# Expert stage with gate and up taken chunk by chunk together

## The chip, the cores and the metric

One core of one Trainium2 chip runs the whole program. The metric is device time in microseconds (us) from start to end of one execution.

## What is computed

The reference runs two layers over 288 tokens, 256 of a prompt and 32 of samples, with 1024 features each. A layer mixes the tokens (retention and a causal convolution) and then sends each token to two of 16 experts. An expert is a gated product with three 1024 x 1024 matrices of its own in float32:

```
ys = (silu(xb @ w_gate[e]) * (xb @ w_up[e])) @ w_down[e]      # for a block xb of tokens
```

The two results of a token are added with the router's weights, scaled by a gate of the layer and added to the residual. The change touches only this expert stage.

## The kernel before

The rows of an expert are taken in blocks of 64 (the kernel's own size), so the 576 pairs of token and expert make 16 experts with one or two blocks each, 35 blocks over both layers. A block is a pass through a loop on each engine; the engines meet at semaphores.

**Weights.** SP loads everything through a ring of twelve slots (line 133). A unit is two chunks of 128 rows of a 1024-wide matrix, 128 x 2 x 1024 floats. Slots 0 to 3 hold gate, 4 to 7 up, 8 to 11 down. SP issues the units in program order and waits for each unit's slot, `freed[s]`, before it issues it (lines 367 to 374). Before the first expert of a layer the same slots hold modulation weights: part 3 in slots 0 to 3 (line 359), part 4 and then part 5 in slots 4 to 7 (lines 360 and 366), w_out in 8 to 11. Slots 4 to 7 are given back by PE in the modulation slab at line 692, late in the mixing stage. After an expert's units SP waits for `routed` and reads the number of its blocks (lines 376 to 378). A slot is given back once per block, and a unit of the next expert waits until the last block of this one has used its slot. Behind the last expert of layer 0, SP loads modulation weights of layer 1 into slots 0 to 7 and convolution weights into 8 to 11 (lines 379 to 387).

**A block on PE** (lines 785 to 834). `half_products` (line 756) is one chunk of one matrix: two matmuls, one for each 512 columns, that write the two halves of a PSUM bank; in float32 each is two instructions. A block is: eight chunks of gate into bank 2; behind the fourth, the combines 0 to 2, which put the result of the block before into banks for DVE to add; eight chunks of up into bank 3, with combine 3 behind the first; `gather` of the next block's rows; the transposes of `hs`, which wait for `h_act`; the transposes of `selT` and `xtok`; eight chunks of down into bank 0. PE gives a slot back behind its last chunk, apart from the last slot of each matrix: ACT gives back slot 3 behind `gate_done` (line 1007) and slot 11 (line 1014), DVE gives back slot 7 behind `up_done` (line 1458).

**ACT and DVE.** ACT takes the sigmoid of gate (line 1008), with a table load before it in each block, then copies rows and results. DVE builds the selections of the next block, takes the combines into the residual (`take`, line 1423), makes the first product of gate and sigmoid (line 1454), then take(3), then the second product with up (line 1460), which signals `h_act`.

In the rows, the helpers stand for most operations: line 406 is every matmul, 409 every transpose, 875 every ACT operation, 374 every load of an expert's unit.

Of the kernel before, what the change touches and what calls it, by code (L numbers as in the profile page):

```python
# [13 lines left out]
KC = D // P  # L14
# [15 lines left out]
UK = 2  # L30
UQ = KC // UK
# [89 lines left out]
def hybrid_step_kernel(nc, x_prompt, x_sample, state_ret, state_conv, c_prompt, c_sample, w_mod, b_mod, g_mix_norm,  # L121
# [6 lines left out]
    with ctx:  # L128
# [99 lines left out]
        xg = cut("moe", 512)  # L228
# [58 lines left out]
        V = type("Signals", (), S)  # L287
# [17 lines left out]
        @block.sync  # L305
        def _(sp):
            mod_v = w_mod.rearrange("l (q k p) c -> l q p k c", q=UQ, p=P)
            in_v = w_in.rearrange("l (q k p) c -> l q p k c", q=UQ, p=P)
            out_v = w_out.rearrange("l (q k p) c -> l q p k c", q=UQ, p=P)
            exp_v = [w.rearrange("l e (q k p) c -> (l e) q p k c", q=UQ, p=P) for w in (w_exp_gate, w_exp_up, w_exp_down)]  # L310

            def row_loads():
                for row, n, src in ((R_GMIX, 8, g_mix_norm), (R_GFFN, 8, g_ffn_norm), (R_BMOD, NMB, b_mod), (R_BCONV, 4, b_conv),
                                    (R_GCLN, 4, g_conv_ln), (R_BCLN, 4, b_conv_ln), (R_GRET, 4, g_ret_gn)):
                    sp.dma_start(vrows[row:row + n, :, :], src.rearrange("l (r p) -> r l p", p=P)).then_inc(in_rows, 16)
                for l in range(L):
                    sp.dma_start(vrows[R_GFIN:R_GFIN + 8, l, :], g_final.rearrange("(r p) -> r p", p=P)).then_inc(in_rows, 16)

            for j in range(2):
                for q in range(UQ):  # L320
                    s = j * UQ + q
                    sp.wait_ge(freed[s], 1)
                    sp.sem_inc(tick, 1)
                    sp.dma_start(ring[:, s], mod_v[0, q, :, :, (1 - j) * D:(2 - j) * D]).then_inc(loaded[s], 16)
                    if s == 1:
                        row_loads()
            blk = sp.alloc_register("blocks_before")
            sp.reg_mov(blk, 0)

            def conv_load(layer, uses):  # L330
                for q in range(UQ):
                    s = G_CONV * UQ + q
                    sp.wait_ge(freed[s], uses(s))
                    sp.sem_inc(tick, 1)
                    sp.dma_start(ring[:, s], in_v[layer, q, :, :, 2 * D:3 * D]).then_inc(loaded[s], 16)

            conv_load(0, lambda s: 1)
            sp.dma_start(cbt[0:120, :, :], state_conv.rearrange("l b t c -> l (b t) c").rearrange("l (r p) c -> l p r c", p=120)[0]) \
                .then_inc(cb_first, 16)
            sp.dma_start(cst[:, NFIRST:], consts[:, NFIRST:]).then_inc(in_const, 16)  # L340
            for l in range(L):

                b0 = sp.snap(blk)
                for j in (G_QK, G_VG):
                    for q in range(UQ):
                        s = j * UQ + q
                        sp.wait_ge(freed[s], unit_uses(s, l, 0, b0))
                        sp.sem_inc(tick, 1)
                        sp.dma_start(ring[:, s], in_v[l, q, :, :, j * D:(j + 1) * D]).then_inc(loaded[s], 16)

                def mod_load(group, k, layer, part):
                    for q in range(UQ):
                        s = group * UQ + q
                        sp.wait_ge(freed[s], unit_uses(s, l, k, b0))
                        sp.sem_inc(tick, 1)
                        sp.dma_start(ring[:, s], mod_v[layer, q, :, :, part * D:(part + 1) * D]).then_inc(loaded[s], 16)

                mod_load(2, 1, l, 2)
                mod_load(0, 1, l, 3)
                mod_load(1, 1, l, 4)  # L360
                for q in range(UQ):
                    s = 2 * UQ + q
                    sp.wait_ge(freed[s], unit_uses(s, l, 2, b0))
                    sp.sem_inc(tick, 1)
                    sp.dma_start(ring[:, s], out_v[l, q]).then_inc(loaded[s], 16)
                mod_load(1, 2, l, 5)
                with sp.Fori(0, E) as e:
                    b = sp.snap(blk)
                    for j in range(3):
                        for q in range(UQ):  # L370
                            s = j * UQ + q
                            sp.wait_ge(freed[s], unit_uses(s, l, PRE[s], b))
                            sp.sem_inc(tick, 1)
                            sp.dma_start(ring[:, s], exp_v[j][bass.ds(l * E + e, 1), q]  # L374
                                         .rearrange("a p k c -> (a p) k c")).then_inc(loaded[s], 16)
                    sp.wait_ge(routed, l + 1)
                    nsub = sp.value_load(nsubi[0:1, bass.ds(e, 1)], min_val=1, max_val=MAXSUB)  # L377
                    sp.reg_add(blk, blk, nsub)
                if l < L - 1:
                    b1 = sp.snap(blk)  # L380
                    for j in range(2):
                        for q in range(UQ):
                            s = j * UQ + q
                            sp.wait_ge(freed[s], unit_uses(s, l, PRE[s], b1))
                            sp.sem_inc(tick, 1)
                            sp.dma_start(ring[:, s], mod_v[l + 1, q, :, :, (1 - j) * D:(2 - j) * D]).then_inc(loaded[s], 16)  # L386
                    conv_load(l + 1, lambda s: unit_uses(s, l, PRE[s], b1))

            yp = y_prompt[0].rearrange("(r p) d -> p r d", p=P)
            sp.wait_ge(mix_open, L + 1)  # L390
            sp.sem_inc(tick, 1)
            sp.wait_ge(fin_cp, 2)
            sp.dma_start(yp[:, :, 0:512], x_tok[:, 0:2, 0:512]).then_inc(y_out, 16)
            sp.wait_ge(fin_cd, 1)
            sp.dma_start(yp[:, 0, 512:D], x_tok[:, 0, 512:D]).then_inc(y_out, 16)
            sp.wait_ge(fin_cp, 4)
            sp.dma_start(yp[:, 1, 512:D], x_tok[:, 1, 512:D]).then_inc(y_out, 16)
            sp.wait_ge(fin_cd, 2)
            sp.dma_start(y_sample.rearrange("b t d -> (b t) d"), x_tok[0:NS, 2, :]).then_inc(y_out, 16)
            sp.wait_ge(y_out, 64)  # L400
# [3 lines left out]
        def _(pe):  # L404
# [65 lines left out]
            for l in range(L):  # L470
# [306 lines left out]
                with pe.Fori(0, E) as e:  # L777
                    nsub = pe.value_load(nsubi[0:1, bass.ds(e, 1)], min_val=1, max_val=MAXSUB)
                    with pe.Fori(0, nsub):
                        pe.reg_add(nn, nn, 1)  # L780

                        def unit(s):
                            pe.wait_ge(loaded[s], l * (16 * LOADS[s]) + e * 16 + 16 * (SETUP[s] + PRE[s] + 1))

                        pe.wait_ge(V.xg_copied, nn)
                        for k in range(KC):
                            s = k // UK
                            if k % UK == 0:
                                unit(s)
                            last = half_products(2, xg, s, k)  # L790
                            if k % UK == UK - 1 and k < KC - 1:
                                last.then_inc(freed[s], 1)
                            if k == 3:
                                pe.wait_ge(V.y_copied, nn)
                                pe.wait_ge(V.selT_copied, nn)
                                for j in range(3):
                                    combine(j).then_inc(V.comb_done, 1)
                        last.then_inc(V.gate_done, 1)

                        for k in range(KC):  # L800
                            s = UQ + k // UK
                            if k % UK == 0:
                                unit(s)
                            last = half_products(3, xg, s, k)
                            if k % UK == UK - 1 and k < KC - 1:
                                last.then_inc(freed[s], 1)
                            if k == 0:
                                pe.wait_ge(V.comb_used, taken)
                                combine(3).then_inc(V.comb_done, 1)
                        last.then_inc(V.up_done, 1)  # L810

                        pe.wait_ge(V.sel_ready, nn)
                        pe.reg_add(taken, taken, 2)
# [228 lines left out]
        def _(dve):  # L1042
# [52 lines left out]
            for l in range(L):  # L1095
# [336 lines left out]
                with dve.Fori(0, nb) as n:  # L1432
# [17 lines left out]
                    for j in range(3):  # L1450
                        dve.wait_ge(V.comb_done, n * 4 + j + 1)
                        take(j)
                    dve.wait_ge(V.sig_done, n + 1)
                    v.tensor_tensor(hs, ps[:, 2, :], gs, ALU.mult).then_inc(V.gated, 1)  # L1454
                    dve.wait_ge(V.comb_done, n * 4 + 4)
                    take(3)
                    dve.wait_ge(V.up_done, n + 1)
                    dve.sem_inc(freed[2 * UQ - 1], 1)
                    dve.wait_ge(V.gated, n + 1)
# [155 lines left out]
```

## Time and profile before

| | us |
|---|---|
| median of three runs (lowest, highest) | 1460.73 (1459.89, 1461.12) |
| the profiled execution | 1459.87 |
| its span | 1457.9 |
| PE busy | 1379.4 (95%) |
| DVE busy | 670.8 (46%) |
| ACT busy | 241.0 (17%) |

The mean rate of all DMA is 344 GB/s. PE's busy time takes in pipelined matmuls whose ends are modelled, so 95% is not a measure of what PE could do at most. All times in the rows count from the start of the span. SPq is the queue in which SP issues DMAs, PEld is the loading of weights into PE.

### The profile page before, as it was taken

To read this page: it belongs to the slowest core of one execution; us is meant where nothing else is said; L and a number is where in the kernel's file an instruction comes from. 1 tells how busy PE (TensorE), PEld (TensorE's weight loads), DVE (VectorE), ACT (ScalarE), POOL (GpSimd) and SP (SyncE) were. 2 spreads that over 40 slices of the span, in tenths; PEclk is the share of its full clock that TensorE was granted. 3 is DMA by queue.
4 is the path that set the end of the run, shared out by engine and by line. 5 is a ranking of instruction groups with operands and counts; after the bars stand their busy time and mean duration, and the time that the engine had idled before them with its cause. 6 is when DMAs were issued, how large, how long until landed. Compare 5 with 4: busy or idle time off the path is not lost.

```text
span 1457.9 us, 20499 instructions
## 1 busy us (share of the span) xinstructions
PE 1379.4 (95%) x7451; PEld 654.2 (45%) x7452; DVE 670.8 (46%) x1955; ACT 241.0 (17%) x400; POOL 92.3 (6%) x142
## 2 busy tenths in 40 slices
PE   6999998999999999999989999899999999999997
PEld 3777654333333343343337766533333333334333
DVE  3598655433333243343346976643343324233343
ACT  2211321111111111111131123211111111111112
POOL 0081010000000000000001710000000000000000
PEclk9999999999999999999999999989999999999999
DMA  9953579999999974999999356799999999899993
GB/s 346 369 196 113 225 267 394 410 410 410 410 410 410 410 296 156 397 410 410 409 410 377 132 186 234 266 358 410 410 410 409 410 410 410 332 392 409 410 409 138
DMA packets 131425, 502.10 MB, mean 344 GB/s; under 512 B 8626, under 2 KB 8946, under 8 KB 131249
## 3 DMA queue, kind: packets, MB, share of 16 engines
q1 hardware_dynamic: 127455, 489.53, 85.2%
q0 software_dynamic: 3456, 10.72, 2.6%
q10 hardware_dynamic: 482, 1.42, 0.3%
q8 instruction: 20, 0.33, 0.1%
q14 instruction: 12, 0.10, 0.0%
HBM read 495.48 MB, written 7.00 MB: 345 GB/s over the span
## 4 chain that ended last, share of the span: by engine, by line
PE 62%; SPq 25%; DMA 5%; issue 3%; DVE 3%; ACT 1%; PEld 1%; PEldq 0%; ACTq 0%; DVEq 0%
PE ps L406 59%; SPq L374 24%; PE ps L409 4%; DMA ring<-in_w_exp_up 3%; DMA ring<-in_w_mod 1%; DMA arena<-in_x_sample 1%; ACT arena L875 1%; SPq L386 1%; DVE hT L1134 0%; SPq L377 0%; DVE stat L1068 0%; DVE rt L1336 0%; PEld ps L406 0%; PEld ps L409 0%; PEldq L466 0%
## 5 line engine op out<-in xcount | busy, mean ns | idle before, releaser
L406 PE MATMUL ps<-ring,arena 128*64 128x512 f32 x3360 | 755.5, 598 | 22.5 <-DMA ring<-in_w_exp_up 15.5
L406 PEld LDWEIGHTS ps<-ring,arena 128*64 128x64 f32 x3360 | 227.5, 137 | 489.4 <-issue 416.6
L875 ACT ACTIVATE arena<-ps 128x512 f32<-128x512 f32 (+3 forms) x238 | 127.8, 551 | 812.0 <-PE ps L406 723.1
L406 PE MATMUL ps<-hT,ring 128*128 128x288 f32 x1024 | 254.2, 409 | 4.3 <-ACT hT L875 2.5
L1426 DVE SCALAR_TENSOR_TENSOR xT<-ps,mod,xT 128x256 f32<-128x256 f32 x280 | 133.1, 475 | 256.2 <-PE ps L406 256.2
L406 PEld LDWEIGHTS ps<-hT,ring 128*128 128x128 f32 x1024 | 194.3, 191 | 63.2 <-issue 7.7
L406 PE MATMUL ps<-arena 64*128 64x288 f32 (+4 forms) x1656 | 206.8, 400 | 4.5 <-DVE xT L1479 1.7
L406 PEld LDWEIGHTS ps<-arena 64*128 64x128 f32 (+4 forms) x1656 | 117.3, 159 | 127.9 <-issue 99.4
L1163 DVE SCALAR_TENSOR_TENSOR arena<-arena,wcT 128x256 f32<-128x256 f32 x240 | 123.5, 576 | 1.6
L875 ACT ACT_TABLE_LOAD x49 | 62.9, 1283 | 302.6 <-PE ps L406 299.1
L1460 DVE TENSOR_TENSOR arena<-ps,arena 128x512 f32<-128x512 f32 x35 | 24.2, 692 | 167.0 <-PE ps L406 167.0
L409 PE MATMUL ps<-cst,arena 128*128 128x128 f32 (+5 forms) x533 | 82.4, 287 | 17.4 <-DMA cst<-in_consts 8.5
L409 PEld LDWEIGHTS ps<-cst,arena 128*128 128x128 f32 (+5 forms) x533 | 59.2, 143 | 48.5 <-issue 24.1
L1454 DVE TENSOR_TENSOR arena<-ps,arena 128x512 f32<-128x512 f32 x35 | 24.2, 692 | 123.2 <-ACT arena L875 123.2
L1462 DVE COPY arena<-ps 128x512 f32<-128x512 f32 x35 | 24.2, 691 | 73.1 <-PE ps L409 73.1
L1428 DVE TENSOR_TENSOR rtmp<-ps,rtmp 128x32 f32<-128x32 f32 x280 | 50.3, 179 | 0.0
L406 PE MATMUL ps<-ring,condT 128*32 128x512 f32 x384 | 44.3, 596 | 3.2 <-DMA ring<-in_w_mod 3.2
L1512 POOL DMA_DIRECT2D out<-in_state_conv x2 | 1.1, 542 | 584.3 <-DVE hT L1139 550.4
L1538 POOL TENSOR_TENSOR arena<-arena,wcT 128x128 f32<-128x128 f32 x62 | 33.5, 572 | 52.5 <-DVE arena L1149 52.0
L1434 DVE TENSOR_SCALAR arena<-cst,slots,wts 128x128 f32<-128x128 f32 x105 | 29.9, 341 | 2.7 <-PE ps L406 1.5
L1436 DVE TENSOR_SCALAR arena<-cst,slots,wts 128x128 f32<-128x128 f32 x105 | 29.9, 341 | 0.0
L406 PEld LDWEIGHTS ps<-ring,condT 128*32 128x32 f32 x384 | 11.2, 110 | 29.2 <-issue 22.9
(169 smaller groups left out, 531.4 us busy)
## 6 DMA issues: line engine op xcount, KB each, us to landing
ring<-in_w_exp_gate SPq DMA_DIRECT2D x128, 1024.0 KB, 17.2
ring<-in_w_exp_up SPq DMA_DIRECT2D x128, 1024.0 KB, 18.1
ring<-in_w_exp_down SPq DMA_DIRECT2D x128, 1024.0 KB, 18.1
ring<-in_w_mod SPq DMA_DIRECT2D x48, 1024.0 KB, 9.5
ring<-in_w_in SPq DMA_DIRECT2D x24, 1024.0 KB, 21.9
ring<-in_w_out SPq DMA_DIRECT2D x8, 1024.0 KB, 12.9
big<-in_state_ret POOLq DMA_DIRECT2D x4, 512.0 KB, 10.3
arena<-in_state_ret POOLq DMA_DIRECT2D x4, 512.0 KB, 5.1
```

The source lines that it names most:

```text
L374: sp.dma_start(ring[:, s], exp_v[j][bass.ds(l * E + e, 1), q] .rearrange("a p k c -> (a p) k c")).then_inc(loaded[s], 16)
L406: return nc.tensor.matmul(out, lhsT, rhs, start=start, stop=stop, skip_group_check=True)
L409: return nc.tensor.transpose(out, in_, ident[0:n, 0:n])
L875: return nc.scalar.activation(out, in_, f, **kw)
L1163: ins = v.scalar_tensor_tensor(cT[:, ct, 0:SEQ], src, wcol, cT[:, ct, 0:SEQ], ALU.mult, ALU.add)
L1426: v.scalar_tensor_tensor(xT[:, c, 0:SEQ], ps[:, bank, 0:SEQ], mod[:, M_GT2 + c, 0:1], xT[:, c, 0:SEQ], ALU.mult, ALU.add)
L1428: last = v.tensor_tensor(rtmp[:, c, :], ps[:, bank, SEQ:T], rtmp[:, c, :], ALU.add)
L1434: v.tensor_scalar(selw[:, t, :], iota, slots[:, 0, t:t + 1], wts[:, 0, t:t + 1], ALU.is_equal, ALU.mult)
L1436: last = v.tensor_scalar(selw1[:, t, :], iota, slots[:, 1, t:t + 1], wts[:, 1, t:t + 1], ALU.is_equal, ALU.mult)
L1454: v.tensor_tensor(hs, ps[:, 2, :], gs, ALU.mult).then_inc(V.gated, 1)
L1460: v.tensor_tensor(hs, ps[:, 3, :], hs, ALU.mult).then_inc(V.h_act, 1)
L1538: last = gp.tensor_tensor(slot[:, k].rearrange("p c (b t) -> p c b t", b=B), win[:, :, :, tap:tap + T_DEC], wc[:, tap * CT:(tap + 1) * CT] ...
```

## The change

SP's loads go in the order gate 0, up 0, gate 1, up 1 and so on, and then down. PE takes chunk k of gate and then chunk k of up. The combines 0 to 2 stand behind the third chunk, combine 3 behind the sixth. On DVE take(3) moves ahead of the first product.

```diff
-                    for j in range(3):
-                        for q in range(UQ):
+                    for j, q in [(j, q) for q in range(UQ) for j in range(2)] + [(2, q) for q in range(UQ)]:
                             s = j * UQ + q
                             sp.wait_ge(freed[s], unit_uses(s, l, PRE[s], b))
...
                         for k in range(KC):
-                            s = k // UK
-                            if k % UK == 0:
-                                unit(s)
-                            last = half_products(2, xg, s, k)
-                            if k % UK == UK - 1 and k < KC - 1:
-                                last.then_inc(freed[s], 1)
-                            if k == 3:
+                            for s, bank, done in ((k // UK, 2, V.gate_done), (UQ + k // UK, 3, V.up_done)):
+                                if k % UK == 0:
+                                    unit(s)
+                                last = half_products(bank, xg, s, k)
+                                if k % UK == UK - 1 and k < KC - 1:
+                                    last.then_inc(freed[s], 1)
+                                if k == KC - 1:
+                                    last.then_inc(done, 1)
+                            if k == 2:
                                 pe.wait_ge(V.y_copied, nn)
                                 pe.wait_ge(V.selT_copied, nn)
                                 for j in range(3):
                                     combine(j).then_inc(V.comb_done, 1)
-                        last.then_inc(V.gate_done, 1)
-
-                        for k in range(KC):
-                            s = UQ + k // UK
-                            if k % UK == 0:
-                                unit(s)
-                            last = half_products(3, xg, s, k)
-                            if k % UK == UK - 1 and k < KC - 1:
-                                last.then_inc(freed[s], 1)
-                            if k == 0:
+                            if k == 5:
                                 pe.wait_ge(V.comb_used, taken)
                                 combine(3).then_inc(V.comb_done, 1)
-                        last.then_inc(V.up_done, 1)
...
+                    dve.wait_ge(V.comb_done, n * 4 + 4)
+                    take(3)
                     dve.wait_ge(V.sig_done, n + 1)
                     v.tensor_tensor(hs, ps[:, 2, :], gs, ALU.mult).then_inc(V.gated, 1)
-                    dve.wait_ge(V.comb_done, n * 4 + 4)
-                    take(3)
                     dve.wait_ge(V.up_done, n + 1)
```

## Rows read from the trace of the kernel before

**Rows 1.** The page's row of DMA share, 40 equal slices of the span.

```profile
DMA  9953579999999974999999356799999999899993
```

**Rows 2.** The chain of waits: start us, us, what.

```profile
490.83 18.59 DMA ring<-in_w_exp_up
...
515.28 25.71 PE ps L406 x136
542.55 25.71 PE ps L406 x136
...
729.64 18.42 DMA ring<-in_w_mod
...
1241.11 18.86 DMA ring<-in_w_exp_up
...
1429.49 7.04 PE ps L406 x32
```

**Rows 3.** Stretches: from:to, length, PE busy, PE clock, DMA share, GB/s.

```profile
200.00:208.00 8.00, 8.00 (x37) 1.00 0.01 3
208.00:224.00 16.00, 11.30 (x118) 1.00 0.92 267
240.00:510.00 270.00, 260.52 (x1379) 1.00 1.03 410
582.00:750.00 168.00, 164.91 (x903) 1.00 1.02 407
956.00:972.00 16.00, 16.00 (x74) 0.92 0.83 290
972.00:1268.00 296.00, 284.93 (x1523) 1.00 1.03 410
```

**Rows 4.** Timeline of PE: start us, us, what, and the wait ahead.

```profile
235.64 3.66 PE L406 MATMUL ps<-ring,arena 128*64 128x512 f32 x16 [1.12 <-ACT arena L875]
...
509.46 1.94 PE L406 MATMUL ps<-ring,arena 128*64 128x512 f32 x8 [0.62 <-DMA ring<-in_w_exp_up]
...
748.10 1.06 PE L406 MATMUL ps<-ring,condT 128*32 128x512 f32 x8 [1.48 <-DMA ring<-in_w_mod]
```

**Rows 5.** Timeline of SP's queue: issues of expert units.

```profile
180.40 5.17 SPq L374 DMA_DIRECT2D ring<-in_w_exp_gate  x4
211.27 5.37 SPq L374 DMA_DIRECT2D ring<-in_w_exp_up  x4
...
524.27 7.36 SPq L374 DMA_DIRECT2D ring<-in_w_exp_gate  x4
...
578.82 7.36 SPq L374 DMA_DIRECT2D ring<-in_w_exp_gate  x4
...
899.45 4.04 SPq L374 DMA_DIRECT2D ring<-in_w_exp_gate  x4
930.31 4.70 SPq L374 DMA_DIRECT2D ring<-in_w_exp_up  x4
```

**Rows 6.** Timeline of one block that PE paces, from gate's last chunk.

```profile
1018.98 0.14 PEld L406 LDWEIGHTS ps<-ring,arena 128*64 128x64 f32 x2 [0.28 <-issue]
...
1020.12 1.28 ACT L875 ACT_TABLE_LOAD   x1 [8.06 <-PE ps L406]
...
1021.42 0.60 ACT L875 ACTIVATE arena<-ps 128x512 f32<-128x512 f32 x1
...
1022.05 0.69 DVE L1454 TENSOR_TENSOR arena<-ps,arena 128x512 f32<-128x512 f32 x1 [3.52 <-ACT arena L875]
...
1025.83 0.14 PEld L406 LDWEIGHTS ps<-ring,arena 128*64 128x64 f32 x2 [0.28 <-issue]
...
1026.68 0.14 PEld L406 LDWEIGHTS ps<-ring,arena 128*64 128x64 f32 x2 [0.29 <-issue]
...
1027.87 0.69 DVE L1460 TENSOR_TENSOR arena<-ps,arena 128x512 f32<-128x512 f32 x1 [4.16 <-PE ps L406]
...
1029.96 0.64 PEld L409 LDWEIGHTS ps<-cst,arena 128*128 128x128 f32 x6 [0.38 <-issue]
```

## The prediction

> **What bounds the kernel now.** I read the page's row of DMA share first: long runs of 9, broken by short dips [rows 1]. The chain of waits says who owns the runs and who owns the dips [rows 2]. It changes hands: a DMA that brings an up unit ends at 509.42, then blocks follow on PE every 27.27 us, then a DMA of the next layer's modulation weights ends layer 0 at 748, then again an up unit (1259.97), then PE to the end. Call X the expert whose last up unit that is; it has two blocks in either layer. The table by stretches gives the reason [rows 3]: from 240 to 510, from 582 to 750 and from 972 to 1268 the stream runs flat at 407 to 410 GB/s. A unit is 128 x 2 x 1024 floats, 1.049 MB, so 2.56 us at that rate; an expert's twelve take 30.7 us, and a block costs PE only 27.27 us. PE starts each expert stage ahead (the ring is filled before it) and loses the lead: it idles 9.5 of 270 us before X in layer 0 and 11.1 of 296 us in layer 1. At X the stream decides; behind X the ring stays full for a block, and PE decides in layer 1 up to the end. In layer 0 both run nearly level, and the stream is last: PE waited 1.48 us for the unit at 748.10 [rows 4].
>
> So two questions price the change: does the stream to X start later, and does the block on PE get longer?
>
> **Part 1, the order of loads.** SP issues in program order and stops at a unit whose slot is taken. Before, the four gate units of the first expert go out at 180.40, and SP then stands until 211.27, when slot 4 (the first up unit's) is given back by the last modulation slab [rows 5]. The transfers of this head start end before 200; from 200 to 208 the stream moves 3 GB/s [rows 3]. Layer 1 shows the same at 899.45 and 930.31 [rows 5]. In the new order the second unit is an up unit, so SP stands there after one gate unit; gate units 2 to 4 wait behind it. Three units, 3 x 2.56 = 7.67 us, move from an empty stretch to behind the wait.
>
> In layer 0 the stream behind the wait has no hole until X: share 0.92 from 208 to 224, where the states are stored, then 1.03 [rows 3]. So 7.67 us arrive at X in full. Block 0 itself isn't held up: it starts at 235.64 [rows 4] and needs its last up unit 12 half-products (10.2 us, part 2) later; seven units behind 211.27 take 17.9 us, with the states' traffic on top about 24 (estimate), so it lands by 236. Bounds: if the deeper queue filled the missing share of those 16 us (0.11 x 16 = 1.8 us), 5.9; at most 7.67. I take 7.67, as the stretch at 1.03 is by far the longer. In layer 1 the stream does run out before expert 1's slots come free: 290 GB/s from 956 to 972 [rows 3], short by (410-290)/410 x 16 = 4.7 us. The late units fill that hole, so 7.67 - 4.7 = 3.0 us remain; bounds 3.0 and 7.67. I take 3.0, because layer 0 shows that a stream with work queued runs at 410 there.
>
> **Part 2, the end of an up unit.** When X's last up unit lands, PE has two half-products left (chunks 6 and 7 of up, the 8 matmuls at 509.46 [rows 4]); in the new order gate 7 stands between them, so three. Two half-products are two pairs of weight loads each, four pairs; the rows at 1025.83 and 1026.68 are two pairs, one half-product, apart: 0.85 us [rows 6]. Plus 0.85 us, once per layer.
>
> **Part 3, the gated product.** Before, gate is done eight half-products before up, and the sigmoid and the first product lie under up. Now gate ends one half-product before up. The rows of one PE-paced block give the new chain [rows 6]. The last weight load of gate at 1018.98 is followed by the table load at 1020.12, 1.14 us later. In the new order the last gate load stands where the row 1025.83 is; the table load then starts at 1026.97, the sigmoid 1.30 later at 1028.27, the first product 0.63 after that at 1028.90. It lasts 0.69, a hand-over on DVE costs 0.03 to 0.04, and the second product lasts 0.69: 1030.32. The transposes of hs would start at about 1030.37 with 0.05 for the hand-over (estimate); they start at 1029.96 now, behind the gather. So PE waits w = 0.41 us per block. Bounds: 0, if the gather hides it, and 0.8, twice my value, if the hand-overs cost more. Nothing below 0: the same matmuls run, and PE has no hole in the block to give back. What waits behind: the transposes of selT and xtok, and the down products, all shifted by w. SP's up slot 7, which DVE returns behind the first product, comes about 3 us later; the stream has a queue by then.
>
> Here the row and a page of the Trainium skill differ. The row has 1.30 us from the table load's start to the sigmoid's. *ScalarE: Activation LUTs*, section "What ACT_TABLE_LOAD costs", states about 1283 ns for the load, as the row shows, plus a drain of about 1380 ns, 2.66 us per switch. By the page w would be 0.41 + 1.38 = 1.79 us; no drain stands between these rows, so the sum goes by the row.
>
> **Part 4, the combines and take(3).** The instructions and the two breaks in the stream of products are the same; they move by some half-products. take(3) now stands before the first product, but DVE is idle 3.52 us before that product and 4.16 us before the second [rows 6], so it costs nothing as long as the fourth combine is ahead of the last four half-products, which it is. A slot of odd rank comes free one half-product (0.85 us) later than before.
>
> **The sum.** Layer 0, by the stream: 7.67 + 0.85 + w for X's first block. The stream then restarts only when slots come free, at 524.27 for the next expert, and, as that has two blocks too, at 578.82 for the one behind [rows 5]: w for X's second block, w for that expert's first, and 0.85 for the slot that comes one half-product later. 7.67 + 0.85 + 0.85 + 3 x 0.41 = 10.6 us. By PE: nine waits to the end of the layer, 7.67 + 0.85 + 3.7 = 12.2, less the 1.48 us that it waited: 10.7. Both agree; 10.6. Layer 1: 3.0 + 0.85 + 7 w (X's first block and six behind it) = 6.7. Together 17.3 us. The profiled execution took 1459.87 us (span 1457.9), 0.9 below the median of the three runs; 1459.87 + 17.3 = 1477.2.
>
> **The rivals.**
> *A faster stream (the other side).* Gate and up alternate, so consecutive units come from two tensors. If that raised the rate, the three flat stretches (270, 168 and 296 us) would shrink; at 420 GB/s, 2.4% more, the gain is 734 x 10/420 = 17.5 us and cancels the forecast, and from there on the change is faster: at 424 GB/s 734 x 14/424 = 24.2 us go, which gives 1453.0. Against it: the rate is 410 to a GB/s in stretches of gate, up and down alike at a share of 1.03 [rows 3]. Beside it, *DMA: Bandwidth & Descriptors*, section "Where 436 GB/s comes from", gives a ceiling of 435 GB/s for the fabric; no row here holds that. Chance 0.04.
> *The late start is hidden.* If slot 4 came free before the head start ends, or the stream had slack up to X, part 1 falls away: 0.85 + 0.85 + 1.2 in layer 0, 3.7 in layer 1, about 1466.5. For it: layer 1's hole. Against it: SP's 31 us of standing in both layers and the flat 410 [rows 3, 5]. Chance 0.1.
> *The sigmoid chain is covered.* w = 0: 7.67 + 0.85 + 0.85 + 3.0 + 0.85 = 13.2, so 1473.1. For it: 0.4 us is a small difference between long chains. Chance 0.15.
> *The table load costs twice.* Now that the sigmoid ends the chain, ACT may need as long again as the load lasts (1.28 us in the row) before it goes on: w = 1.69. Layer 0 then goes by PE, 7.67 + 0.85 + 9 x 1.69 - 1.48 = 22.3, layer 1 gives 3.0 + 0.85 + 7 x 1.69 = 15.7: 1497.9. Against it: the sigmoid starts 0.02 us behind the load's end [rows 6]. By the page named in part 3 this would be the outcome, at about 1499. Chance 0.05.
>
> **How the numbers follow.** The forecast has 0.62, and 0.04 is for what I don't see. Low end: w = 0 with the lower bound of part 1 in layer 0, 1473.1 - 1.8 = 1471. High end: the upper bound of layer 1 (4.7 more) with w = 0.8 (about 4 more): 1486. Left out are the hidden start, the double load and the faster stream, two in ten. A change below 0.2%, 2.9 us, can't be told from none here. Faster 0.04 (the first rival), within 0.2% 0.03, slower 0.93.
>
> **What would show it.** In SP's queue, one gate issue near 180 and near 900 and the other three behind 211 and 930; an empty stream from about 192 to 208. X's last up unit landing 7 to 8 us later in layer 0, and some 3 us more than layer 0's end shift in layer 1. Blocks of 27.7 us in the stretches that PE paces, and transposes whose idle time is ended by DVE's second product. The prediction is wrong if those blocks stay at 27.27, if X's unit lands on time, or if the flat rate leaves 410.

## The result

| | before | changed |
|---|---|---|
| median us (lowest, highest; runs) | 1460.92 (1459.89, 1464.48; 4) | 1479.76 (1476.44, 1480.63; 4) |
| ratio, 95% interval | | 1.0127 [1.0111, 1.0142] |
| profiled execution, span | 1459.87, 1457.9 | 1480.63, 1478.2 |

The changed kernel is slower by 1.3%, some 16 to 21 us. The forecast was 1477.2 in a range of 1471 to 1486.

SP's queue in the changed kernel shows the head start cut to one unit in both layers, and from the restart on the issues in pairs. It answers to [rows 5].

```profile
180.55 0.38 SPq L373 DMA_DIRECT2D ring<-in_w_exp_gate  x1
211.53 0.38 SPq L373 DMA_DIRECT2D ring<-in_w_exp_up  x1
212.17 1.50 SPq L373 DMA_DIRECT2D ring<-in_w_exp_gate  x1
...
589.50 0.38 SPq L373 DMA_DIRECT2D ring<-in_w_exp_gate  x1
590.26 0.37 SPq L373 DMA_DIRECT2D ring<-in_w_exp_up  x1
...
911.15 0.38 SPq L373 DMA_DIRECT2D ring<-in_w_exp_gate  x1
942.01 0.38 SPq L373 DMA_DIRECT2D ring<-in_w_exp_up  x1
```

The stretches of the changed kernel, columns as in [rows 3]: the stream is empty from 192 on, where it moved 380 GB/s from 192 to 200 before. Layer 1 runs 11.7 us later in the changed kernel (942.01 against 930.31), so the hole from 956 to 972 (290 GB/s before) would lie at 968 to 984 here; the stretch around it shows it filled.

```profile
192.00:200.00 8.00, 8.00 (x37) 1.00 0.01 5
200.00:208.00 8.00, 8.00 (x37) 1.00 0.00 0
240.00:510.00 270.00, 253.19 (x1343) 1.00 1.03 410
965.00:985.00 20.00, 19.13 (x106) 1.00 1.03 409
```

PE idles 16.8 of 270 us before X in layer 0, where it idled 9.5: the rate is the same, the stream is later. The chain of waits of the changed kernel, against [rows 2]:

```profile
498.57 18.59 DMA ring<-in_w_exp_up
...
524.28 22.56 PE ps L405 x108
551.97 22.56 PE ps L405 x108
579.65 22.56 PE ps L405 x108
...
1256.38 18.64 DMA ring<-in_w_exp_up
...
1448.24 7.04 PE ps L405 x32
```

X's last up unit lands at 517.16 instead of 509.42 and, in layer 1, at 1275.02 instead of 1259.97. Behind X blocks follow every 27.68 us instead of 27.27. The modulation unit that ended layer 0 before is no longer in the chain. One block that PE paces, against [rows 6], shows what was put into each:

```profile
1036.09 0.14 PEld L405 LDWEIGHTS ps<-ring,arena 128*64 128x64 f32 x2 [0.28 <-issue]
...
1037.23 1.28 ACT L866 ACT_TABLE_LOAD   x1 [14.90 <-PE ps L405]
...
1038.53 0.60 ACT L866 ACTIVATE arena<-ps 128x512 f32<-128x512 f32 x1
1039.16 0.69 DVE L1447 TENSOR_TENSOR arena<-ps,arena 128x512 f32<-128x512 f32 x1 [3.65 <-ACT arena L866]
...
1039.88 0.69 DVE L1451 TENSOR_TENSOR arena<-ps,arena 128x512 f32<-128x512 f32 x1
...
1040.63 0.64 PEld L408 LDWEIGHTS ps<-cst,arena 128*128 128x128 f32 x6 [0.79 <-DVE arena L1451]
```

Gate's last weight load, the table load 1.14 us later, the sigmoid 1.30 after that, both products back to back on DVE, and the transposes directly behind the second. Their idle time is now ended by DVE, not by PE's own stream.

### The profile page after: what moved, and what is told of

The parts are those of the page before. It is cut to its first block, busy times and chain, and to the rows that moved or that the text cites. A ratio compares the mean times of both kernels' runs of the same rounds, so it can differ in the third digit from the quotient of the medians.

```text
span 1478.2 us, 20499 instructions
## 1 busy us (share of the span) xinstructions
PE 1382.9 (94%) x7451; PEld 657.1 (44%) x7452; DVE 674.0 (46%) x1955; ACT 241.1 (16%) x400; POOL 92.3 (6%) x142
## 4 chain that ended last, share of the span: by engine, by line
PE 57%; SPq 27%; DVE 5%; ACT 4%; DMA 3%; issue 3%; PEld 1%; PEldq 0%; ACTq 0%; DVEq 0%
PE ps L405 53%; SPq L373 26%; PE ps L408 4%; DMA ring<-in_w_exp_up 3%; ACT L866 2%; ACT arena L866 2%; DVE arena L1447 1%; DVE arena L1451 1%; DMA arena<-in_x_sample 1%; SPq L376 0%; DVE hT L1125 0%; DVE stat L1059 0%; DVE rt L1327 0%; PEld ps L405 0%; PEld ps L408 0%
```

## The experiments

All ratios are to the kernel before, run on the same chip beside it.

**Order of loads off.** The changed kernel, with the first expert of each layer loaded in the old order and the others by turns.

```diff
+                b = sp.snap(blk)
+                for j, q in [(j, q) for j in range(3) for q in range(UQ)]:
...
-                with sp.Fori(0, E) as e:
+                with sp.Fori(1, E) as e:
```

> The changed kernel, but SP loads the first expert of each layer in the old order (four gate units, four up, four down); all other experts and PE as changed. Theory (the order of loads costs 7.7 us in layer 0 and 3.4 in layer 1, because three units of the head start move behind SP's wait for slot 4): the gates go out together near 180, X's last up unit lands at 509 to 510 again, and of the 19 us about 10 go, so about 1469 to 1470. Blocks stay at 27.69. Rival (the stream catches up, and the 19 us are the longer end of every block): no change, 1477 to 1480.

Measured 1467.39 us, 1.0041 [1.0025, 1.0056]. PE's timeline at X:

```profile
510.83 2.79 PE L415 MATMUL ps<-ring,arena 128*64 128x512 f32 x12 [0.51 <-DMA ring<-in_w_exp_up]
513.45 2.49 PE L415 MATMUL ps<-arena 128*64 128x256 f32 x24
516.28 1.64 PE L418 MATMUL ps<-cst,arena 128*128 128x128 f32 x11 [0.34 <-DVE arena L1461]
...
543.96 1.63 PE L418 MATMUL ps<-cst,arena 128*128 128x128 f32 x11 [0.34 <-DVE arena L1461]
```

The unit is back at 510.8, the blocks are still 27.68 long and wait for DVE. So two thirds of the loss go with the loads of one expert per layer, and the rival, that the stream catches up, falls. The time is some 2 us below the expectation; what makes the difference was not followed.

**Order of loads alone.** The kernel before, with only the first expert of each layer loaded by turns.

```diff
+                b = sp.snap(blk)
+                for j, q in [(j, q) for q in range(UQ) for j in range(2)] + [(2, q) for q in range(UQ)]:
...
-                with sp.Fori(0, E) as e:
+                with sp.Fori(1, E) as e:
```

> The kernel before, but SP loads the first expert of each layer in the new order; nothing else. Theory (order of loads by itself): 7.5 us later at X in layer 0 and 3.4 more in layer 1, blocks of 27.27: about 1472. Rival (the stream catches up): 1460 to 1462.

Measured 1471.94 us, 1.0067 [1.0047, 1.0087].

```profile
516.42 1.94 PE L415 MATMUL ps<-ring,arena 128*64 128x512 f32 x8 [0.63 <-DMA ring<-in_w_exp_up]
518.19 2.49 PE L415 MATMUL ps<-arena 128*64 128x256 f32 x24
520.61 1.63 PE L418 MATMUL ps<-cst,arena 128*128 128x128 f32 x11
...
547.88 1.63 PE L418 MATMUL ps<-cst,arena 128*128 128x128 f32 x11
```

The unit is 7.0 us late (SP went on at 210.34 in this run, 0.9 us earlier than in the kernel before), the blocks are 27.27 long and nothing waits for DVE. Eight matmuls follow the unit as before, not twelve.

**Gate one chunk further ahead.** The changed kernel; PE takes gate 0, gate 1, up 0, gate 2, up 1 and so on.

```diff
-                        for k in range(KC):
-                            for s, bank, done in ((k // UK, 2, V.gate_done), (UQ + k // UK, 3, V.up_done)):
...
+                        for k in range(KC + 1):
+                            if k < KC:
+                                part(0, 2, k, V.gate_done)
+                            if k > 0:
+                                part(UQ, 3, k - 1, V.up_done)
```

> The changed kernel with gate one chunk further ahead of up (gate 0, gate 1, up 0, gate 2, up 1, ..., gate 7, up 6, up 7); loads as changed. Theory (the sigmoid chain starts one half-product too late, w = 0.41 us, and X's end has one half-product too many, 0.85 us): blocks of 27.27 again, two half-products behind X's last up unit, X's unit as late as in the changed kernel; 1.9 us go in layer 0 and 3.7 in layer 1, about 1474. Rival (the waits come from taking gate and up by turns as such, or from take(3) ahead of the product): blocks stay near 27.7, 1477 to 1480.

Measured 1472.2 us, 1.0059 [1.0039, 1.0079].

```profile
513.95 4.51 PE L405 MATMUL ps<-ring,arena 128*64 128x512 f32 x20 [0.66 <-DMA ring<-in_w_exp_gate]
518.29 2.49 PE L405 MATMUL ps<-arena 128*64 128x256 f32 x24
520.71 1.63 PE L408 MATMUL ps<-cst,arena 128*128 128x128 f32 x11
...
547.99 1.63 PE L408 MATMUL ps<-cst,arena 128*128 128x128 f32 x11
```

Blocks of 27.28, no wait for DVE. Taking the two matrices by turns costs nothing in itself, nor does take(3) ahead of the product: this kernel has both. Not as expected, PE stops for the last gate unit and not for the last up unit; the five half-products behind it cover the up unit's landing. The time is 1.8 us below the expectation.

**Up ahead of gate.** The changed kernel, with up first in each chunk: the same suspected cost, increased.

```diff
-                            for s, bank, done in ((k // UK, 2, V.gate_done), (UQ + k // UK, 3, V.up_done)):
+                            for s, bank, done in ((UQ + k // UK, 3, V.up_done), (k // UK, 2, V.gate_done)):
```

> The changed kernel with up ahead of gate in each chunk, so gate ends the phase. Theory: the sigmoid chain starts one half-product later still, w = 0.41 + 0.86 = 1.27 us, blocks of 28.55; behind X's last up unit four half-products instead of three. Layer 0 goes by PE, 8.6 us more, layer 1 6.9 more: about 1495. Rival (w is a fixed cost of the hand-overs, not set by where gate ends): no change from 1480.

Measured 1492.49 us, 1.0204 [1.0181, 1.0227].

```profile
516.26 3.65 PE L405 MATMUL ps<-ring,arena 128*64 128x512 f32 x16 [0.66 <-DMA ring<-in_w_exp_up]
519.75 2.49 PE L405 MATMUL ps<-arena 128*64 128x256 f32 x24
523.43 1.63 PE L408 MATMUL ps<-cst,arena 128*128 128x128 f32 x11 [1.20 <-DVE arena L1451]
...
551.98 1.63 PE L408 MATMUL ps<-cst,arena 128*128 128x128 f32 x11 [1.20 <-DVE arena L1451]
```

Blocks of 28.55, sixteen matmuls behind the unit, the wait for DVE longer by 0.86: one half-product on each count, as the theory has it. The time came out 2.5 us below the expectation; 0.9 of it is there when PE meets X's last up unit (516.26 against 517.20 in the changed kernel).

**Both off.** The changed kernel with the first expert's old order and gate one chunk further ahead (the edits of the first and the third experiment together).

> The changed kernel with both: first expert of each layer loaded in the old order, and gate one chunk further ahead on PE. Theory (order of loads, X's end and the sigmoid chain are all that the change costs): back to the kernel before within 2 us, 1459 to 1463. Rival (something of the mixing itself costs): 1464 or more.

Measured 1461.24 us, 0.9995 [0.9981, 1.0010]: the kernel before, within the interval. So the order of the first expert's loads and the place where gate ends, with the third half-product, account for the loss.

**An earlier start.** The kernel before, with the first expert loaded gate, down, up.

```diff
+                b = sp.snap(blk)
+                for j, q in [(j, q) for j in (0, 2, 1) for q in range(UQ)]:
...
-                with sp.Fori(0, E) as e:
+                with sp.Fori(1, E) as e:
```

> The kernel before, but the first expert of each layer is loaded gate, down, up, so that SP goes on with slot 8, which PE gives back some 3 us before slot 4. Theory (the start of the stream behind SP's wait sets the time in layer 0, and in layer 1 the hole before expert 1 takes the gain): 2 to 3 us faster, about 1458. Rival (the start of the stream does not matter, or up lands too late for block 0): 1461 or more.

Measured 1460.16 us, 0.9991 [0.9979, 1.0002]: a gain is not shown. SP's queue did start earlier, 207.49 instead of 211.27, but 1.0 of these 3.8 us is not the edit's: in this run the gates went out at 179.40 instead of 180.40, and block 0 began at 234.70 instead of 235.64. The unit of X landed at 508.45, 1.0 earlier as well, so the head start of 2.8 us gave nothing there. Block 0 did not wait for up. The stretches of this kernel show the stream behind 236:

```profile
232.00:236.00 4.00, 2.08 (x14) 1.00 1.02 408
236.00:240.00 4.00, 4.00 (x26) 1.00 0.99 354
240.00:244.00 4.00, 4.00 (x22) 1.00 1.00 363
244.00:248.00 4.00, 4.00 (x22) 1.00 0.90 341
```

SP has issued all twelve units by 222 and waits for block 0 to give the first slot back at 236.90, and the stream thins out; before, it ran at 410 in these stretches. From 236 to 248 this costs 4 x (56 + 47 + 69)/410 = 1.7 of the 2.8 us; the rest lies ahead of 236 and was not followed. So in layer 0 the stream was as early as the ring allows: starting later costs in full (7.74 us for 7.67), and starting 2.8 us earlier gave nothing at X.

**Meant to beat both.** Gate one chunk further ahead on PE, first expert gate, down, up, all other experts by turns.

> A kernel meant to beat both: the changed kernel with gate one chunk further ahead on PE, the first expert of each layer loaded gate, down, up, all others by turns. Theory: no w, no third half-product, the stream behind the wait starts some 3 us earlier, and the restart at two-block experts moves 403 to 410 GB/s in its first 12 us instead of 360 to 380, which is worth 1.3 us; but expert 1's slots bound the early start in both layers and PE's blocks bound the rest: 1458 to 1461, 0 to 3 us below the kernel before. Rival (up now comes too late for block 0, because gate and up are taken together): 1462 or more.

Measured 1461.35 us, 1.0008 [0.9995, 1.0021]. That is just above the range expected. Its blocks are 27.28 long as expected, but its block 0 ran at a granted clock of 0.50 up to 240 and the stream moved 238 GB/s from 236 to 240, where the kernel with the earlier start had 354. No version was shown to beat the kernel before.

## Why the prediction was right, and where a size was off

The first three rows are the terms, the five behind them add up to the last.

| part | forecast, us | measured, us |
|---|---|---|
| X's last up unit, layer 0 | 7.67 | 517.16 - 509.42 = 7.74 |
| half-product behind it, per layer | 0.85 | 0.86 |
| w per block | 0.41 | 27.68 - 27.27 = 0.41 |
| end of layer 0 (first products of layer 1) | 10.6 | 771.71 - 762.08 = 9.6 |
| from there to the first up issue of layer 1 | 0 | 942.01 - 930.31 - 9.6 = 2.1 |
| X's last up unit, layer 1, on top | 3.0 | 15.05 - 11.70 = 3.35 |
| X to the last down products, layer 1 | 3.72 | 18.75 - 15.05 = 3.70 |
| behind them | 0 | 20.3 - 18.75 = 1.6 |
| sum | 17.3 | 20.3 (spans) |

**Part 1 (order of loads)** held in both layers, size included. In layer 0 the stream has no hole up to X [rows 3], so the delay of its start arrives in full; the hole in layer 1 took 4.3 of the 7.67 us, 4.7 were forecast.

**Part 2 (the end of an up unit)**: in the changed kernel the gather starts 2.63 us behind the first matmul of the last up unit, where it started 1.77 behind. The four matmuls more are in this row, against the eight of [rows 4]:

```profile
517.20 2.80 PE L405 MATMUL ps<-ring,arena 128*64 128x512 f32 x12 [0.51 <-DMA ring<-in_w_exp_up]
519.83 2.49 PE L405 MATMUL ps<-arena 128*64 128x256 f32 x24
```

**Part 3 (the gated product)**: each link has the duration that [rows 6] gave it, and w is 0.41. The page *ScalarE: Activation LUTs* of the Trainium skill (section "What ACT_TABLE_LOAD costs") has a drain of about 1380 ns for every switch to a different set of functions. The trace does not agree, and the load's own 1.28 us is the page's. The sigmoid starts 1.30 us behind the start of the load in the changed kernel too, where that chain ends the wait. From block to block the load before was for the sigmoid too, so the set may be the same. But where the mixing stage of the changed kernel goes from the square root to the sigmoid, the load starts at 158.66, 0.02 us behind the operation ahead of it, and the sigmoid at 159.95, 1.29 us later. The rival of a load that costs twice falls, as w is 0.41.

A side remark of part 3 was off. Up's slot 7 is given back ahead of the second product, and this starts 2.93 us behind up's last weight load where it started 1.19 behind: at most 1.7 us later, not about 3; nothing rested on it.

**Part 4 (combines and take(3) at no cost)**: shown by the kernel with gate further ahead, which keeps both and has blocks of 27.28.

**The sum for layer 0** was off by 1.0 us, and both of its ways were mis-sized. By PE I took off 1.48 us for its wait at the end; the timeline of the kernel before has a second one 2.5 us earlier. The last row is where layer 1's first products start.

```profile
745.56 1.07 PE L406 MATMUL ps<-ring,condT 128*32 128x512 f32 x8 [0.69 <-DMA ring<-in_w_mod]
...
762.08 15.76 PE L406 MATMUL ps<-hT,ring 128*128 128x288 f32 x64 [1.28 <-ACT hT L875]
```

In the changed kernel PE meets neither:

```profile
755.20 3.64 PE L405 MATMUL ps<-ring,condT 128*32 128x512 f32 x32
...
771.71 17.16 PE L405 MATMUL ps<-hT,ring 128*128 128x288 f32 x64 [1.87 <-ACT hT L866]
```

So PE ended the layer, not the stream. The last down products of the layer begin 12.26 us late (745.67 against 733.41), as forecast by PE (12.2), and the first matmul behind the two waits 9.68 us late (758.98 against 749.30): the waits hid 2.6 us, not 1.48. By the stream I had the restart right (589.50 - 578.82 = 10.7 against 10.6) but not what followed: see the last section.

The ratios of the two kernels with one half off add up to 1.0% and not 1.27%; their intervals leave room for that. The waits at the end of the layer are not the reason. Behind them the kernel with the first expert's old order is 3.31 us late and the one with gate further ahead 6.52 (752.61 and 755.82 against 749.30), together 9.83, where the changed kernel is 9.68 late.

**The upper end of the range** was too low by its own terms. With w = 0.8 layer 0 goes by PE: 7.67 + 0.85 + 9 x 0.8 - 1.48 = 14.2, 3.6 over 10.6, and layer 1 has 2.7 more, so 6.3 us stand where "about 4" was taken. The result does not hang on it.

**The 2.1 and 1.6 us** were not foreseen. They stand in stretches that the change does not touch, and the granted clock differs there. Each fence has the start of layer 1 and then the end of the program, for the changed kernel and then for the kernel before:

```profile
771.00:789.00 18.00, 17.30 (x67) 0.91 1.02 389
1456.00:1470.00 14.00, 8.25 (x32) 0.88 0.00 0
```

```profile
762.00:778.00 16.00, 15.92 (x68) 1.00 1.02 386
1437.00:1450.00 13.00, 6.56 (x32) 1.00 0.00 0
```

At the start of layer 1 the same 64 matmuls took 17.16 us instead of 15.76: the granted clock was 0.50 (1.2 GHz) from 772 to 774 in the changed kernel. At the end the same 16 matmuls took 5.84 us instead of 4.15, at 0.50 from 1461 to 1464. What decides it is open. PE had idled 1.87 us ahead of the 64 matmuls instead of 1.28, but that alone does not decide it: with 1.28 us ahead they took 17.85 us with the order of loads alone, 17.92 with gate further ahead and 18.22 with both off, a kernel that is as fast as the one before. The 1.4 us lie within what the runs of one kernel differ by (4.6 us before, 4.2 changed). The profiled execution of the kernel before is at the low end of its runs and that of the changed kernel at the high end, so the medians, 18.8 us apart, are nearer to the forecast of 17.3 than the spans.

**The rivals.** The faster stream: the flat stretches stay at 410 GB/s, so no. The hidden late start: no, by the first two experiments. The covered chain: no, by the wait for DVE, which grows by one half-product in the fourth experiment and is gone in the third.

## What to carry to other kernels

SP issues its loads in the order of the program, and in the changed kernel it stood from 180.55 to 211.53 at a unit whose slot was taken, with three units behind it whose slots were free. When an order of loads is changed, look at each place where the queue enters the loop: what could go out early before, and what stands in front of it now. Where two results are joined, let the one with the longer chain behind it end first; one half-product of lead (0.86 us) was worth 0.41 us per block here.

## What was not expected

**The restart.** When the ring has run dry at a two-block expert, the stream comes up faster in the order by turns. The first 12 us from 2 us behind the first issue, for the kernel before and then for the changed one:

```profile
580.82:592.82 12.00, 12.00 (x62) 1.00 0.98 367
```

```profile
591.50:603.50 12.00, 12.00 (x64) 1.00 1.02 410
```

The three kernels that load the other experts in the old order have 359, 367 and 380 GB/s in that stretch, the six that load by turns 391 to 410. At 410 against 367 that is 12 x 43/410 = 1.3 us in favour of the change. In SP's queue of the changed kernel the second unit goes out 0.76 us behind the first; that pairs of slots come free together is the likely reason, but no run tried it by itself.

**The clock in block 0.** The first block of layer 0 ran at a granted clock of 1.00 (2.4 GHz) from 236 on in the kernel before and in the changed one, and at 0.50 (1.2 GHz) up to 240 in three others. In every kernel PE had idled 4.0 us until about 225, so that alone doesn't tell them apart; the cause is open. In the kernel with the first expert's old order the first 24 matmuls took 7.52 us instead of the changed kernel's 5.37, the slot of gate 0 came free at 240.83 instead of 238.84, and the stream thinned out:

```profile
236.00:240.00 4.00, 4.00 (x12) 0.50 0.84 334
240.00:244.00 4.00, 4.00 (x24) 1.00 0.52 146
```

X's unit landed at 510.8 there, not at 509.4 as in the kernel before. The likely reason is that the stream carried the gap at the start of the stage to its end; no run tried the clock by itself.
